# GpSimd no longer makes low parts of weight tiles in the two mixers: VectorE makes all of them

## What is computed

```
h = rmsnorm(x, g_mix[l])
dq, dk, dv, c_q, c_kv_kr, xq, gate_logits = split(h @ w_in[l])
y_diff = diff_attention(dq, dk, dv, ...) @ w_diff_o[l]      # 8 heads of 2 softmax maps each
y_mla  = latent_attention(c_q, c_kv_kr, ...) @ w_mla_o[l]   # 8 heads
y_mem  = memory_cross_attention(xq, mem_n, ...) @ w_cross_o[l]  # 4 heads
merged = gates[0] * y_diff + gates[1] * y_mla + gates[2] * y_mem
x = x + merged @ w_out[l]
```

## Time and profile before

| what | value |
|---|---|
| median of 3 runs | 2480.88 us |
| the profiled execution | 2485.56 us, its span 2484.2 us |
| TensorE busy | 2396.5 us, 96% of the span |
| VectorE busy | 1521.6 us, 61% |
| ScalarE busy | 1187.6 us, 48% |
| GpSimd busy | 283.8 us, 11% |
| mean granted TensorE clock | 0.988 |

### The profile page before, as it was taken

The page is one execution under the profiler, slowest core; times in us unless marked ns, Lnnn a source line. Parts: engine busy times, 40 slices in busy tenths (PEclk is TensorE's granted clock), DMA queues, the critical chain, the costliest instruction groups (busy, mean ns, idle before and its releaser), DMA issues.

```text
span 2484.2 us, 34969 instructions
## 1 busy us (share of the span) xinstructions
PE 2396.5 (96%) x14214; PEld 2060.9 (83%) x14214; DVE 1521.6 (61%) x2325; ACT 1187.6 (48%) x1782; POOL 283.8 (11%) x247
## 2 busy tenths in 40 slices
PE   8998999889999999999999998999999998999999
PEld 8986787779979977777898786787998876887997
DVE  6555556776556657666655677655665686656654
ACT  4443454344444445444444455554554555554543
POOL 1100010000000000000000121333100122333000
PEclk9999999999999999999999999999999999999999
DMA  7754544446656555544566554445566553445564
GB/s 225 198 200 152 165 127 139 126 146 193 187 171 186 181 192 177 170 137 152 166 183 212 180 170 129 119 126 166 175 196 203 181 156 117 119 144 161 168 187 146
DMA packets 269424, 411.69 MB, mean 166 GB/s; under 512 B 13770, under 2 KB 141658, under 8 KB 269264
## 3 DMA queue, kind: packets, MB, share of 16 engines
q1 hardware_dynamic: 262400, 389.59, 51.5%
q0 software_dynamic: 6432, 19.28, 2.9%
q10 hardware_dynamic: 432, 0.59, 0.1%
HBM read 408.31 MB, written 1.10 MB: 165 GB/s over the span
## 4 chain that ended last, share of the span: by engine, by line
PE 76%; DVE 14%; ACT 6%; issue 2%; POOL 1%; DMA 0%; SPq 0%; ACTq 0%; DVEq 0%
PE banks L1605 14%; PE banks L1607 14%; PE banks L1606 13%; PE banks L1631 10%; PE banks L1640 9%; PE banks L1632 9%; DVE w_lo L2186 3%; ACT w_hi L1884 3%; PE banks L1754 1%; DVE probs L2373 1%; ACT probs L1992 1%; PE banks L1694 1%; PE banks L1707 1%; POOL stat L2873 1%; DVE mx_merged L2861 1%
## 5 line engine op out<-in xcount | busy, mean ns | idle before, releaser
L2186 DVE TENSOR_TENSOR w_lo<-w_raw,w_hi 128x1024 fp32r<-128x1024 f32 x688 | 837.7, 1224 | 706.2 <-ACT w_hi L1884 703.8
L1884 ACT ACTIVATE w_hi<-w_raw 128x1024 fp32r<-128x1024 f32 (+2 forms) x744 | 776.2, 1049 | 569.1 <-PE banks L1607 420.5
L1631 PE MATMUL banks<-xt_hi,w_hi 128*128 128x256 f32 x1920 | 477.9, 287 | 12.2 <-ACT xt_hi L1914 8.9
L1632 PE MATMUL banks<-xt_hi,w_lo 128*128 128x256 f32 x1920 | 475.4, 282 | 0.0
L1605 PE MATMUL banks<-w_hi,xt_hi 128*128 128x512 f32 (+2 forms) x1088 | 450.7, 414 | 12.1 <-DVE xt_lo L2214 4.4
L1607 PE MATMUL banks<-w_hi,xt_lo 128*128 128x512 f32 (+2 forms) x1088 | 430.2, 395 | 0.0
L1606 PE MATMUL banks<-w_lo,xt_hi 128*128 128x512 f32 (+2 forms) x1088 | 429.9, 395 | 0.0
L1631 PEld LDWEIGHTS banks<-xt_hi,w_hi 128*128 128x128 f32 x1920 | 364.2, 190 | 16.2 <-issue 12.6
L1632 PEld LDWEIGHTS banks<-xt_hi,w_lo 128*128 128x128 f32 x1920 | 367.3, 191 | 0.0
L1640 PE MATMUL banks<-xt_lo,w_hi 128*128 128x256 f32 x1920 | 270.3, 283 | 0.0
L1605 PEld LDWEIGHTS banks<-w_hi,xt_hi 128*128 128x128 f32 x1088 | 208.6, 192 | 60.2 <-issue 8.3
(11 more groups left out here) (399 smaller groups left out, 2825.7 us busy)
## 6 DMA issues: line engine op xcount, KB each, us to landing
w_raw<-in_w_mlp SPq DMA_DIRECT2D x128, 512.0 KB, 3.7
w_raw<-in_w_in SPq DMA_DIRECT2D x104, 512.0 KB, 3.7
w_raw<-in_ffn_w_gate SPq DMA_DIRECT2D x88, 512.0 KB, 4.0
w_raw<-in_ffn_w_up SPq DMA_DIRECT2D x88, 512.0 KB, 4.1
w_raw<-in_ffn_w_down SPq DMA_DIRECT2D x88, 512.0 KB, 3.6
w_raw<-in_attn_w_in SPq DMA_DIRECT2D x72, 512.0 KB, 3.8
w_raw<-in_ret_w_in SPq DMA_DIRECT2D x64, 512.0 KB, 3.8
w_raw<-in_ret_w_out SPq DMA_DIRECT2D x16, 512.0 KB, 3.7
```

What stands on the lines that cost most here:

```text
L1631: pe.matmul(out[f], hi[:, cols], xh, start=(c == 0), stop=False)
L1632: pe.matmul(out[f], lo[:, cols], xh, start=False, stop=False)
L1884: act.activation(k.w_hi[i % SPLIT][:, 0:m], k.raw[i % RAW][:, 0:m], ACT.Copy).then_inc(*ev.mark(k.w_hi_made, ("w_hi", i)))
L2186: dve.tensor_tensor(lo, raw, hi.bitcast(F32), ALU.subtract).then_inc(*ev.mark(k.w_lo_made, ("w_lo", i)))
```

## The change

One line is taken out, so `self.share` stays 0 in the mixers. The step "split" of the 56 tiles then goes to VectorE's program at L2186 in place of GpSimd's at L2892; its place in the plan is the same.

```diff
         def outputs():
             yield from need("qt", "kt", "v")
-            self.share = 2
             yield from attend("diff", 2, diff_done)
             yield from need("cqt")
             yield from attend("cross", 2, divided("cross", o_cross, CROSS_D, 2, 2 * DIFF_H + MLA_H))
```

## The result

The kernel with the change took 2500.44 us (median of 4 executions, 2498.37 to 2502.86) beside 2480.51 us before (4 executions): a ratio of 1.0081 [1.0064, 1.0098], or 20 us more (16 to 24). Slower was the likeliest side, but the forecast was +9.8 us, and 2500.4 lies just past the upper end of its range. The profiled execution took 2498.37 us (span 2497.1), 12.9 us of span more than before's.

A forecast was written before the change was run, and what follows sets the result against it. TensorE's matmuls were taken to bound the kernel, with the change moving only its waits. Per mixer 1.4 + 2.3 + 1.3 - 0.1 = 4.9 us, 9.8 for two, on 2480.9 gave 2490.7 us; range 2479 to 2500.

The forecast's parts named there:

- diff heads, 1525 to 1570: First mixer's diff heads: VectorE's waits for `w_hi` and its low parts, less removed lengthenings, delay TensorE by 1.4 us.
- diff heads' end, 1570 to 1610: First mixer: VectorE falls up to 1.3 us further behind, but slack and rounds without maxima absorb it: 0.
- cross heads, to 1646: First mixer from 1610: VectorE waits for `w_hi` and makes the low part before reducing, so exponentials come late: +2.3 us.
- latent heads, to 1675: First mixer from 1646: rounds of 4.9 us against TensorE's 4.46 build a lag that reaches the exponentials at 1662.89: +1.3 us.
- merges: Mixer's merges and their end: additions into `merged` shorten, but TensorE waits only for the last ones: -0.1 us.
- the mechanism: Mixers' attention: the closed loop of VectorE and ScalarE, low part ahead of the next maxima, delays TensorE; 2490.7 us, chance 0.58.
- the four steps at ScalarE's exponentials: Diff heads, 1525 to 1570: four successive low parts formerly GpSimd's shift the chain by +2.3, -1.0, +1.9 and -1.8 us.
- all other stages as before: Sign of being right: mixers some 5 us longer each, while every stage outside them keeps its length.
- the clock: TensorE's clock may dip more or less often after waits, putting a mixer 1 to 3 us off either way.
- Absorbed: Mixers do as well as the dilated attention; added waits and removed lengthenings cancel: 2480 to 2485 us, chance 0.26.
- Faster: Lengthenings go and low parts fit VectorE's idle time: 3.4 us gained a mixer, 2474.1 us, chance 0.09.
- Loop-bound throughout: Every low part beside attention in both mixers costs its 1.15 us: 2525 us, or 2503 for half; chance 0.07.

The follow-up runs named there:

- Run 6: The changed kernel with VectorE's low part queued behind the next head's maxima, in the mixers' attention only: 2469.14 us, 0.9937 of the kernel before.
- run 1: The changed kernel measured again without any edit, against the kernel before: 2501.3 us beside 2483.13, ratio 1.0062.
- run 5: The kernel before with GpSimd's 56 low parts left out altogether and no added wait in VectorE: 2468.99 us, 0.995 of the kernel before.
- run 2: The kernel before, GpSimd still making its low parts, but VectorE also waits for those tiles' `w_hi`: 2504.12 us, 1.0076 of the kernel before.
- run 8: The changed kernel with low parts behind the next maxima in all stages with attention: 0.9895 of before from three executions; two more took 4696.15 and 6181.59 us.

## Why the prediction was off, step by step

Shifts of TensorE's transpositions of probabilities, after against before, each counted from the shift at its mixer's first one (-1.86 us in the first mixer, +5.46 in the second):

| step | forecast | first mixer | second mixer |
|---|---|---|---|
| diff heads, 1525 to 1570 | +1.4 | +1.47 | +1.0 |
| diff heads' end, 1570 to 1610 | 0 | +0.76 | +1.45 |
| cross heads, to 1646 | +2.3 | +2.44 | +2.44 |
| latent heads, to 1675 | +1.3 | +1.96 | +1.96 |
| merges | -0.1 | 0 | 0 |
| behind the mixer | 0 | +0.66 | +0.5 |
| sum | +4.9 | +7.3 | +7.4 |

**Right: the mechanism and its two large terms.** In the diff heads the four steps at ScalarE's exponentials came out at +2.2, -0.96, +2.06 and -1.8, against +2.3, -1.0, +1.9 and -1.8 forecast. In the cross heads the exponentials start 2.2 us later, as forecast (1622.46 after, 1619.90 before, the offset now +0.37), and the second wait (2.39) is the one named. All lengthened instructions are at their medians; all additions into `merged` take 0.69 us, where every second one took up to 2.78. Run 6 settles that the place of the low part in VectorE's queue is the cause: the wait moves behind the maxima, and the loss turns into a gain.

The forecast was 9.8 us and the time 20 above before, 15.4 in the second measurement: the steps that failed are the following.

**Failed: "Diff heads' end, 1570 to 1610: 0".** I took the lag for covered by the slack between an exponential and its transposition. But the transposition at 1588.64 waits for something else, the bank that VectorE empties into `mx_gate` at 1587.84, behind a low part and 1.41 us long: 1.04 us, where it waited 0.29 before. The slack that I had read belonged to another wait. In the second mixer this comes again (0.73). The other 0.72 there is no lag of the change: TensorE waits 0.52 us for VectorE's division and 0.44 for a copy of ScalarE's at 2121 to 2123, as it does in the first mixer of both kernels (0.51 and 0.45 before), and only before's second mixer lacks these waits, since its granted clock had been lowered just ahead of them, from 2108.9 us on. The same stretch is why that mixer's diff heads show +1.0; the transposition itself stood at +1.85.

**Failed in size and place: "Latent heads, 1646 to 1675: +1.3".** It was 1.96, and not at the exponentials of 1662.89, where the forecast had it: the transposition of those has no wait after the change either. VectorE at the first latent heads, after:

```profile
1649.45 1.23 DVE L2185 TENSOR_TENSOR w_lo<-w_raw,w_hi 128x1024 fp32r<-128x1024 f32 x1 [2.37 <-ACT w_hi L1883]
1650.60 1.22 DVE L2675 TENSOR_TENSOR mx_qt<-mx_qt,stat 128x1024 f32<-128x1024 f32 x1
1651.73 0.48 DVE L2372 CUSTOM_DVE_ANT_0 probs<-banks,causal,head_scale 128x256 f32<-128x256 f32 x1
...
1654.86 1.23 DVE L2185 TENSOR_TENSOR w_lo<-w_raw,w_hi 128x1024 fp32r<-128x1024 f32 x1 [2.37 <-ACT w_hi L1883]
```

I had reckoned with an average round. Here the new low part stands ahead of the norm's product of 128 x 1024; before, that product ran at 1644.19, right behind the maxima of the head before and with no wait. Now the product, and with it the maxima, come late: TensorE waits 0.67 us for their exponentials at 1653.65, where it had no wait, and is 0.8 us later. At 1660.71 it waits 0.55 us for a bank that VectorE empties (`mx_diff_t_lo`), again something else than exponentials.

**Missed: what follows behind each mixer.** Another 0.5 to 0.7 us come there, which "all other stages as before" did not allow for. The last of the 28 low parts now stands in VectorE's queue at 1754.15, ahead of the additions into `x` and of `tok` (the next norm): TensorE waits for `tok` 0.99 us at 1756.76 and 0.67 at 1758.09, where before it waited 0.98 once, at 1752.39.

**Named, not priced: the clock.** I had left it as 1 to 3 us either way. It may have a side: in the mixers' attention of before, after and run 1 it fell to its lower level at the end of waits of TensorE (1.9 to 2.7 us long) or just behind them, so more waits may mean more such stretches. Mean granted clock was 0.9880 over the six executions of run 1 and 0.9892 over the 17 of the kernel before beside them; one stretch of 3.41 us lowers the mean by 3.41 x 0.5 / 2484 = 0.0007, so that would be 1.7 stretches, an estimate of some 3 us of the 15.4. Single executions scatter by more (0.986 to 0.991), so this side isn't shown.

**The sum.** 7.3 + 7.4 in and behind the mixers, less 1.9 before the first one, gives the 12.9 us between the two spans. The rest of the first measurement's 20 us is the draw of executions: before's profiled execution took 5.0 us more than the median, after's 2.1 us less. With 17 executions of the kernel before and 6 of the changed one the difference was 15.4 by the ratio (18.2 by the medians), near the 14.7 in and behind the mixers; of these 9.8 were forecast and 4.9 are the missed and undersized terms.

**The rivals.** *Absorbed* fell, and so did half of its reason: the dilated stage stays full only in the stretch that I had looked at. *Faster* had a real mechanism with too low a price: I gave the lengthened instructions 3.4 us a mixer at most, and run 5 shows 12.4 us for both, 6.2 each. What it got wrong is that the low parts fit into idle time: that idle time is a wait of an engine that serves its queue in order, and cannot be filled by work behind it. The rule of the Trainium skill on the shared read port (SBUF — State Buffer, "Who interferes with whom"), by which whichever engine starts first holds up the other, showed in both directions: in run 2 a low part of GpSimd's took 3.42 us in place of 2.39 beside a product of VectorE's that had begun 0.06 us before it. The 12.4 us that it is worth here are less than the 31 of the order. The prediction's reading that the lengthened instructions have both inputs in SBUF was too narrow: the `TENSOR_SCALAR` at 1637.32 has one and took 1.07 us in place of 0.17, and a copy in run 2 took 2.62 in place of 0.43. *Loop-bound throughout* at half its price (2503) is near the time, yet not by its mechanism: between the marked places TensorE caught up or stayed level.

**Open.** Why run 8's kernel had two very long executions in one set and none in the next; and why a wait of 2.39 us left the clock alone in after while one of 2.40 at the same place in run 1 did not.

## What to carry to other kernels

When two engines serve each other in rounds (here maxima to exponentials, and `w_hi` to low part), put on each in-order queue first what the other engine waits for, and last what has four tiles of slack; "idle before X" is not room for more work if X itself heads the queue. Handing work from an idle engine to a busier one takes its interference away but also closes rounds that had been open, so price three things apart: interference gone, waits added, work added (here -12, +9 and +19 us, the work's second half dearer than its first). And for each lag ask of every resource of the next round (exponentials, banks, copies) how much slack it has: the one with the least is where it comes out.

## What the runs showed of the hardware

One GpSimd instruction of 2.4 us can hold up a VectorE instruction of almost no size: two on 8 columns took 2.46 us in run 2 in place of 0.24. Not every one does: the 28 GpSimd low parts of a mixer lengthened 9 VectorE instructions by 15.5 us before, and 11 by 18.4 us in run 2, where both engines were released by the same `w_hi`. The maxima, which read a bank, kept their 0.48 us beside them. In the mixers' attention the granted clock fell for 3.41 us at a time, 3 times before and 4 after, and each fall cost at most 1.7 us of matmuls.
